# Experts with a second size of tail: 64 rows on two column groups of TensorE, beside 32 rows on four

## The reference

```python
logits = hf @ w_router + b_router;  top_val, top_idx = lax.top_k(logits, 4)
gu  = lax.ragged_dot(xs, w_gu, group_sizes) + b_gu[e]          # 1024 -> 2048
act = gate * sigmoid(1.702 * gate) * (up + 1)                  # gate and up clamped at 7
out = lax.ragged_dot(act, w_down, group_sizes) + b_down[e]     # 1024 -> 1024
y   = segment_sum(out * prob, token)
```

```
 79 155  99 160 155 146  93 132 | 134 122 191 150 161 127 214  96
129 100 143 124  64 152 147 122 | 114 152  91 115 122 105 162 168
```

## Time and profile before

| | us |
|---|---|
| median of three runs | 2581.58 |
| the profiled execution | 2580.96 |
| its span in the profile | 2579.4 |

### The profile page before, as it was taken

One profiled execution on the slowest core, in us unless ns is written; L12 is line 12 of the kernel. 1 busy time (PEld: TensorE's weight loads), 2 busy tenths in 40 slices (PEclk: granted clock), 3 DMA queues, 4 the chain that ended last, 5 costly groups with the idle time before them and its releaser, 6 DMA issues. The chain is left out here.

```text
span 2579.4 us, 36293 instructions
## 1 busy us (share of the span) xinstructions
PE 2373.8 (92%) x11130; PEld 1553.7 (60%) x11131; DVE 1391.8 (54%) x1996; ACT 1117.1 (43%) x1443; POOL 566.2 (22%) x843
## 2 busy tenths in 40 slices
PE   8589999999986399999999999999999999999965
PEld 1177677777754256556567566766575666676641
DVE  0124554545333566556466666766565575766647
ACT  0023333333221345445455455555454554555532
POOL 0122333333211312112112121221121212121110
PEclk9799999999687699999999999999999999999985
DMA  8840000000020787778689889988797797999945
GB/s 307 330 173 34 33 33 33 27 14 23 29 66 12 290 320 286 264 277 318 251 313 344 312 319 371 343 317 313 293 335 301 258 362 277 350 343 368 350 161 222
DMA packets 142977, 604.43 MB, mean 234 GB/s; under 512 B 20129, under 2 KB 25262, under 8 KB 104470
## 3 DMA queue, kind: packets, MB, share of 16 engines
q1 hardware_dynamic: 120311, 551.51, 55.0%
q0 software_dynamic: 21968, 50.99, 8.1%
q10 hardware_dynamic: 662, 1.50, 0.2%
HBM read 561.82 MB, written 42.30 MB: 234 GB/s over the span
## 5 line engine op out<-in xcount | busy, mean ns | idle before, releaser
L1710 DVE TENSOR_TENSOR lo<-raw,hi 128x1024 fp32r<-128x1024 f32 x600 | 716.6, 1222 | 200.1 <-ACT hi L1645 173.2
L1645 ACT ACTIVATE hi<-raw 128x1024 fp32r<-128x1024 f32 x600 | 613.1, 1054 | 172.4 <-PE pg L1595 172.4
L1529 PE MATMUL py<-raw,aT 128*128 128x512 f32 x1184 | 537.9, 599 | 6.3 <-ACT aT L1657 6.3
L1592 PE MATMUL pg<-hi,xs 128*128 128x512 f32 x1184 | 467.3, 395 | 0.0
L1593 PE MATMUL pg<-lo,xs 128*128 128x512 f32 x1184 | 465.3, 393 | 0.0
L1595 PE MATMUL pg<-hi,xs 128*128 128x512 f32 x1184 | 367.3, 392 | 0.0
L1529 PEld LDWEIGHTS py<-raw,aT 128*128 128x128 f32 x1184 | 214.5, 190 | 250.2 <-issue 238.0
L1592 PEld LDWEIGHTS pg<-hi,xs 128*128 128x128 f32 x1184 | 222.9, 188 | 68.9 <-issue 20.1
L1595 PEld LDWEIGHTS pg<-hi,xs 128*128 128x128 f32 x1184 | 222.8, 188 | 49.2
L1593 PEld LDWEIGHTS pg<-lo,xs 128*128 128x128 f32 x1184 | 223.1, 188 | 47.4
L392 PE MATMUL X<-hT,w_in 128*128 128x128 f32 (+1 forms) x1728 | 223.8, 289 | 0.8 <-issue 0.8
(11 more groups left out here) (295 smaller groups left out, 2581.0 us busy)
## 6 DMA issues: line engine op xcount, KB each, us to landing
raw<-in_w_gu SPq DMA_DIRECT2D x300, 1024.0 KB, 7.3
raw<-in_w_down SPq DMA_DIRECT2D x148, 1024.0 KB, 6.9
wada<-in_w_ada SPq DMA_DIRECT2D x12, 2048.0 KB, 7.7
w_in<-in_w_in SPq DMA_DIRECT2D x5, 2048.0 KB, 14.1
moe_rows<-zero SPq DMA_DIRECT2D x9, 512.0 KB, 11.6
x<-in_x_prompt SPq DMA_DIRECT2D x8, 512.0 KB
w_out<-in_w_out SPq DMA_DIRECT2D x1, 4096.0 KB, 25.0
xr<-in_x_prompt SPq DMA_DIRECT2D x8, 512.0 KB, 3.7
```

Of the source, the lines that this page charges most:

```text
L1529: return pe.matmul(py[n][:, :], aT[:, kt, :], raw[KT + kt // 2][:, kt % 2, n * 512:(n + 1) * 512], start=(kt == 0), stop=(kt == KT - 1))
L1592: pe.matmul(pg[u][b][:, :], xs[:, kt, 0, :], wh[:, u, :], start=False, stop=False)
L1645: act.activation(hi[q % RING][:, :, :], grain(q), ACT.Copy).then_inc(s["hi"], 1)
L1710: dve.tensor_tensor(lo[q % RING][:, :, :], grain(q), hi[q % RING][:, :, :].bitcast(F32), ALU.subtract).then_inc(s["lo"], 1)
```

## The change

`TAILS = (32, 64)`: a tail is of class 1 up to 32 rows and of class 2 up to 64, IDLE becomes 3. An expert with 161 to 192 rows is now one item. A 64-row tail runs on two column groups of 64: group g makes 512 gate columns into py0 and 512 up columns into py1, so there are two matmuls (u) for each group in bias and up-projection, and two of 512 columns for each kt of the down-projection. Every engine has a third body, chosen by a second comparison. GpSimd loads the tail's slots in both arrangements (four copies of 32, two of 64), keeps both, and gathers always 64 rows of the tail. `act_t` moves into the upper half of `act1`; three waits are added for that and for py1. Cut to its core:

```diff
-TAIL = 32
+TAILS = (32, 64)
+TAIL = max(TAILS)
...
-IDLE = 2
+IDLE = 1 + len(TAILS)
...
-            dve.tensor_scalar(ic[0:M, 9:10], ic[0:M, 5:6], float(ITEM + TAIL), None, ALU.is_gt).then_inc(s["im1"], 1)
+            dve.tensor_scalar(ic[0:M, 10:11], ic[0:M, 5:6], float(ITEM + TAILS[0]), None, ALU.is_gt)
+            dve.tensor_scalar(ic[0:M, 9:10], ic[0:M, 5:6], float(ITEM + TAIL), float(len(TAILS)), ALU.is_gt, ALU.mult).then_inc(s["im1"], 1)
             dve.wait_ge(s["im1"], 8)
+            dve.tensor_tensor(ic[0:M, 7:8], ic[0:M, 7:8], ic[0:M, 10:11], ALU.add)
             dve.tensor_tensor(ic[0:M, 8:9], ic[0:M, 8:9], ic[0:M, 9:10], ALU.subtract).then_inc(s["im1"], 1)
             dve.wait_ge(s["im1"], 9)
             dve.tensor_tensor(ic[0:M, 7:8], ic[0:M, 7:8], ic[0:M, 8:9], ALU.add).then_inc(s["im1"], 1)
...
+        xs_t = sb("xs_t", [P, KT * TAIL])
...
+        act_t = act1[:, 512:1024]
...
-                                body(i, False)
+                                body(i, 0)
                             with eng.Else():
-                                body(i, True)
+                                with eng.If(cls < 2):
+                                    body(i, TAILS[0])
+                                with eng.Else():
+                                    body(i, TAILS[1])
+
+        def part(T, u):
+
+            return slice(None) if T == TAILS[0] else u
+
+        def per_group(T):
+
+            return T * FF // P
...
+                for T, rows in zip(TAILS, (idx_t, idx_u)):
+                    for g in range(P // T):
+                        pool.dma_start(rows[g * T:(g + 1) * T, :], scratch["slots"][bass.ds(first + P, T), :]).then_inc(s["idx"], 16)
...
-                                        bass.IndirectOffsetOnAxis(ap=idx_t[0:TAIL, 0:1], axis=0)).then_inc(s["xg_t"], 16)
+                                        bass.IndirectOffsetOnAxis(ap=idx_u[0:TAIL, 0:1], axis=0)).then_inc(s["xg_t"], 16)
...
-                pool.tensor_copy(nxt_t[:, :], idx_t[:, :]).then_inc(s["nxt"], 1)
+                pool.tensor_copy(nxt_t[:, :], idx_t[:, :])
+                pool.tensor_copy(nxt_u[:, :], idx_u[:, :]).then_inc(s["nxt"], 1)
...
+                    pool.indirect_dma_start(scratch["acc"][:, :], bass.IndirectOffsetOnAxis(ap=now_u[0:tail, 1:2], axis=0),
+                                            act1[0:tail, :], None, compute_op=ALU.add).then_inc(s["y_out"], 16)
...
+            def tail_bias(T):
+                W = per_group(T)
+                for u in range(W // 256):
+                    for g in range(P // T):
+                        pe.matmul(py[u][g * T:(g + 1) * T, :], sel[:, 0:T].bitcast(F32),
+                                  bgu[:, :].rearrange("e (u n) -> e u n", u=2)[:, part(T, u), g * W:(g + 1) * W].bitcast(F32), start=True, stop=False)
+
+            def tail_up(kt, T):
+                W = per_group(T)
+                for u in range(W // 256):
+                    for g in range(P // T):
+                        last = pe.matmul(py[u][g * T:(g + 1) * T, :], xs_t[:, kt * T:(kt + 1) * T], raw[kt][:, part(T, u), g * W:(g + 1) * W],
+                                         start=False, stop=(kt == KT - 1))
                 return last
...
-                for c in range(2):
+                for c in range(per_group(T) // P):
                     last = pe.transpose(pg[0][0][:, c * P:(c + 1) * P], act_t[:, c * P:(c + 1) * P], identm[:, :])
...
+            def tail_down(kt, T):
+                W = per_group(T)
+                g, c = kt // (W // P), kt % (W // P)
+                for n in range(P // T):
+                    last = pe.matmul(pg[1][0][n * T:(n + 1) * T, 0:W], aT_t(T)[:, c, g * T:(g + 1) * T],
+                                     raw[KT + kt // 2][:, kt % 2, n * W:(n + 1) * W], start=(kt == 0), stop=(kt == KT - 1))
                 return last
...
+                    tail_rows(i, tail)
...
                         pe.wait_ge(s["xt"], i + 1)
                         pe.wait_ge(s["y0"], i + 1)
+                        pe.wait_ge(s["y1"], i + 1)
                         pe.sem_inc(s["met"], 1)
-                        tail_bias()
+                        tail_bias(tail)
...
+                    T, W = tail, per_group(tail)
+                    for n in range(P // T):
+                        last = act.activation(act1[0:T, n * W:(n + 1) * W], pg[1][0][n * T:(n + 1) * T, 0:W], ACT.Copy)
                     last.then_inc(s["y_t"], 1)
...
+                if tail and b:
+                    dve.wait_ge(s["aTt_ps"], i + 1)
...
+                gate_ps = py[0][:, 0:W]
+                up_ps = py[0][:, W:2 * W] if T == TAILS[0] else py[1][:, :]
+                weight = (now_t if T == TAILS[0] else now_u)[:, 2:3].bitcast(F32)
                 dve.wait_ge(s["gt_mm"], i + 1)
-                dve.tensor_scalar(gate[:, 0:W], py[0][:, 0:W], LIMIT, None, ALU.min).then_inc(s["gate_t"], 1)
-                dve.tensor_scalar(up[:, 0:W], py[0][:, W:2 * W], -LIMIT, LIMIT, ALU.max, ALU.min).then_inc(s["up_t"], 1)
+                dve.wait_ge(s["y_out"], i * 32 + 32)
+                dve.tensor_scalar(gate[:, 0:W], gate_ps, LIMIT, None, ALU.min).then_inc(s["gate_t"], 1)
+                dve.tensor_scalar(up[:, 0:W], up_ps, -LIMIT, LIMIT, ALU.max, ALU.min).then_inc(s["up_t"], 1)
...
-                dve.scalar_tensor_tensor(out=gate[:, 0:W], in0=gate[:, 0:W], scalar=now_t[:, 2:3].bitcast(F32), in1=sig[:, 0:W],
+                dve.scalar_tensor_tensor(out=gate[:, 0:W], in0=gate[:, 0:W], scalar=weight, in1=sig[:, 0:W],
                                          op0=ALU.mult, op1=ALU.mult).then_inc(s["glu_t"], 1)
...
-                dve.scalar_tensor_tensor(out=act_t[:, :], in0=up[:, 0:W], scalar=1.0, in1=gate[:, 0:W],
+                dve.scalar_tensor_tensor(out=act_t[:, 0:W], in0=up[:, 0:W], scalar=1.0, in1=gate[:, 0:W],
                                          op0=ALU.add, op1=ALU.mult).then_inc(s["act_t"], 1)
```

More of the change, by code:

```diff
@@ L1458, in load_slots @@
                 pool.dma_start(idx[:, :], scratch["slots"][bass.ds(first, P), :]).then_inc(s["idx"], 16)
-                for g in range(4):
-                    pool.dma_start(idx_t[g * TAIL:(g + 1) * TAIL, :], scratch["slots"][bass.ds(first + P, TAIL), :]).then_inc(s["idx"], 16)
+                for T, rows in zip(TAILS, (idx_t, idx_u)):
+                    for g in range(P // T):
+                        pool.dma_start(rows[g * T:(g + 1) * T, :], scratch["slots"][bass.ds(first + P, T), :]).then_inc(s["idx"], 16)
             def gather(item):
-                pool.wait_ge(s["idx"], item * 80 + 80)
+                pool.wait_ge(s["idx"], item * 112 + 112)
                 pool.sem_inc(s["met"], 1)
@@ L1535, in tail_rows @@
                 for kt in range(KT):
-                    last = pe.transpose(pt[0][:, kt * TAIL:(kt + 1) * TAIL], xg_t[:, kt * P:(kt + 1) * P], identm[0:TAIL, 0:TAIL])
+                    last = pe.transpose(pt[0][:, kt * T:(kt + 1) * T], xg_t[0:T, kt * P:(kt + 1) * P], identm[0:T, 0:T])
                 last.then_inc(s["xt_ps"], 1)
[L1539 to L1542, removed]
@@ L1553, in tail_act @@
                     last = pe.transpose(pg[0][0][:, c * P:(c + 1) * P], act_t[:, c * P:(c + 1) * P], identm[:, :])
                 last.then_inc(s["aTt_ps"], 1)
[L1556 to L1559, removed]
-                                     raw[KT + g][:, c, n * W:(n + 1) * W], start=(kt == 0), stop=(kt == KT - 1))
+            def tail_down(kt, T):
[4 more added lines that the diff above has]
+                                     raw[KT + kt // 2][:, kt % 2, n * W:(n + 1) * W], start=(kt == 0), stop=(kt == KT - 1))
@@ L1599, in item @@
                 if tail:
-                    tail_act(i)
+                    tail_act(i, tail)
                 transpose_rows(i + 1, 0)
@@ L1661, in item @@
                     act.wait_ge(s["xt_ps"], i + 1)
-                    act.activation(xs_t[:, :, :], pt[0][:, 0:KT * TAIL].rearrange("p (k t) -> p k t", k=KT), ACT.Copy).then_inc(s["xt"], 1)
+                    act.activation(xs_t[:, 0:KT * tail], pt[0][:, 0:KT * tail], ACT.Copy).then_inc(s["xt"], 1)
                 for q in range(RING, GRAINS):
@@ L1669, in item @@
                     act.wait_ge(s["gate_t"], i + 1)
-                    act.activation(sig[:, 0:W], gate[:, 0:W], ACT.Sigmoid, scale=ALPHA).then_inc(s["sig_t"], 1)
+                    act.activation(sig[:, 0:per_group(tail)], gate[:, 0:per_group(tail)], ACT.Sigmoid, scale=ALPHA).then_inc(s["sig_t"], 1)
                 squash(i, 0)
@@ L1676, in item @@
                     act.wait_ge(s["aTt_ps"], i + 1)
[L1677 removed]
+                    act.activation(aT_t(tail), pg[0][0][:, 0:per_group(tail)].rearrange("p (c t) -> p c t", t=P), ACT.Copy).then_inc(s["aT_t"], 1)
                 squash(i, 1)
@@ L1686, in item @@
                     act.wait_ge(s["yt_mm"], i + 1)
-                    for n in range(4):
```

(6 more changed lines are left out.)

45 lines of the change are left out of this document (20 added, 25 removed).

## The result

The changed kernel takes 2552.24 us (median of four, 2550.29 to 2555.35) against 2581.79 us (2580.42 to 2586.19): ratio 0.9884 [0.9867, 0.9901], 29.5 us less. Forecast were 2534.4 us and a range up to 2544. The profiled execution is the slowest of the four, 2555.35 us, span 2553.8.

What follows compares the result with a forecast made beforehand. TensorE was taken as the bound, with transfers close behind in plain items. Items -311.5 + 4 x 64.9 = -51.9 us, plus 1.0 start, 0.2 plan, 4.1 end: -46.6 from 2580.96 gives 2534.4 us, range 2527.5 to 2544.

Steps and rivals of the forecast that it cites:

- The 12 items with 32-row tails and the 17 plain ones I leave at their lengths: Expert phase: unchanged item classes stay at 53.09 and 38.94 us, since the second comparison runs ahead in TensorE's queue.
- My sign for stretches that have grown: Between GpSimd's stores: stretches of 53.1 or 38.9 us that have grown would prove the forecast wrong at the cover.
- the cover in the new item: 64-row item: VectorE's longer tail activation for b = 0 still ends 0.8 us before TensorE comes for it.
- The new item: Each of four 64-row items takes 64.9 us, between 64.5 and 65.3, with its two column groups running side by side.
- The 0.6 for wider copies and transpositions: 64-row item: 0.2 us each for more activation transpositions, wider row transpositions and ScalarE's wider copy.
- The bound of two groups in turn: 64-row item: groups run one after the other, 87.3 us an item and 2624 us in all; chance 5%.
- the stalls: New item: the cover fails or a copy is late by 1 to 3 us, adding 4 to 12 us; chance 11%.
- The rival in the prediction: Changes of item class: third body fetched at 19 changes, 7.1 us each, 135 us more, 2669 us; chance 1%.
- GpSimd ahead of the first item: Before the first gather: two more small transfers cost 0 to 3.9 us, taken as 1.0; hidden in later items.
- The end: Behind the last store: four more idle steps of 1.03 us, 4.1 us, with 0 as lower bound.
- The rival that gave it 22%: End of the phase: GpSimd's drain swallows the added idle steps, giving 2530.3 us; chance 22%.
- The first item and the plan: Start: two more plan operations cost 0.2 us; the first item was forecast to gain 0.

Runs made afterwards that it cites:

- e5: Changed kernel with xs alone moved back to 192 modulo 256, its remainder in the kernel before; 2540.64 us.
- e2: Kernel before with xs alone shifted by 32 bytes, by unused tensors before and behind it; 2595.95 us.
- e8: Kernel before with GpSimd's part of the change alone (64-row lists, copies, gather), xs kept at 192 modulo 256; 2580.95 us, ratio 0.9999.
- e3: Changed kernel with items walked in groups of 24 instead of 8, so 16 reads instead of 11 behind the last store; 2562.3 us.
- e6: Changed kernel with xs moved by pads to remainder 0 modulo 256; 2539.05 us in one profiled execution.
- e15: Changed kernel with xs at 0 modulo 256, run again and timed; 2534.43 us, ratio 0.9812.
- e1: Changed kernel with xs 32 bytes further, at a multiple of 64 bytes, by one unused tensor; 2552.09 us, ratio 0.9874.
- e10: Changed kernel with xs at 0 modulo 256, groups of 36, and the 128-row gather waiting for its own list only; 2521.99 us, ratio 0.9762.

## Why the prediction missed

**Which step failed.** "The 12 items with 32-row tails and the 17 plain ones I leave at their lengths." They grew by 0.37 to 0.40 us, which makes 12 x 0.38 = 4.6 us, 15 x 0.40 = 6.0 us, and 2.0 us for the one of 40.96: the whole gap of 12.6 us between the stores. I argued from instructions and waits, and both were right for these items, but for one stall (below); what changed was the address of an operand, which no view of the profile and no line of the diff about matmuls shows. By the sums of the stretches in the changed kernel and in e5 the address is worth 1532.54 - 1520.55 = 12.0 us, the four new items with it; the stall and a new item priced too high nearly cancel in what is left. My sign for stretches that have grown pointed at the cover in the new item, and it was not that. e2 puts it into the kernel before, e5 takes it out of the changed one. Where it acts can be seen in both traces: from the bias of a plain item to the transposition of its activation stand 1590.93 - 1569.85 = 21.08 us before and 1654.78 - 1633.32 = 21.46 after. That is the whole 0.38, over the 90 matmuls of the up-projection between them 4 ns each (the other six of an item's 96 stand ahead of this bias).

```profile
1569.85 0.63 PE L1578 MATMUL pg<-bgu,sel 128*128 128x512 f32 x2
...
1590.93 0.60 PE L1525 MATMUL pt<-ident,actm 128*128 128x128 f32 x4
```

```profile
1633.32 0.63 PE L1604 MATMUL pg<-bgu,sel 128*128 128x512 f32 x2
...
1654.78 0.60 PE L1546 MATMUL pt<-ident,actm 128*128 128x128 f32 x4
```

(Before, then after; each in order of time.)

**Items: right.** 33 stores, with expert 10 among the four, as counted.

**The new item: right in kind, its number by luck.** 64.9 us forecast, 64.88 to 64.94 measured; but at the distance of before it is 64.53 to 64.59 (e5). The sum over a plain item was 22.4 + 3.0 + 0.6 = 26.0 us; it is 64.53 - 38.94 = 25.6. The 0.6 for wider copies and transpositions was too much by 0.4, and the place put 0.38 back. The bound of two groups in turn, 87.3 us, is refuted, as are the stalls: cover 0.96 us where I gave 0.8. The share of the transfers is 0.63 where I gave 0.56, with TensorE busy in all but 0.4 us of the stretch.

**The third body: one stall, once.** A stall of 1.35 us stands where TensorE first leaves a body with a tail for the plain one:

```profile
983.97 0.70 PE L1604 MATMUL pg<-bgu,sel 128*128 128x512 f32 x2 [1.35 <-issue]
```

The item costs 40.96 - 39.37 = 1.6 us over a later plain one behind a tail, once. Every kernel with the third body has the stall at this place, 1.0 to 1.8 us long, and none without it. It is a fetch of instructions, by the times of the packets on that queue (24 of 16 KB in the changed kernel, 18 before). One starts at 982.8 us and takes 0.88; TensorE's first load of the plain body, after 2.15 us of standing idle, is at 983.94. From there to the end of the phase only three more come, at 1374.9, 1395.4 and 1422.0, all in the first item with a 64-row tail, and they delay nothing that shows; the kernel before and e8 have none after 925.0 and 925.8 until the phase is over. The trace doesn't say whose instructions a packet holds; but by their times a fetch comes with the first entry into a body and with the first return to the plain one, and never again. The rival in the prediction had the mechanism, but 19 times and at 7.1 us. All later changes of class cost at most 0.06 us: 39.37 behind a tail, 39.31 behind none. The Trainium skill (Runtime: NRT & Kernel Launch, Instruction fetch mechanics) would have a stall at each branch out of the two pages held; this trace shows it at the first only.

**GpSimd ahead of the first item.** Forecast 1.0 with 0 to 3.9, measured 1.9 (e8 alone: 1.9). The issue was right, at 1.07; "transfers in flight together mostly land together" was not quite: the wait grew by 0.75 us.

**The end.** Forecast 4.1, came 9.1. Two terms were mis-sized. An idle step costs 1.17 us, not 1.03, and seven were right: with the steps about them 5.6 us. Why a step is longer stays open: in e8, without the third body, an idle item still takes 1.03 us but an idle group 1.18. The other 3.4 us are the drain, which I had as fixed or as shrinking, and which grew. The rival that gave it 22%, that it swallows the steps, falls by e3.

**The first item and the plan.** 2.3 and 0.7 us over. The 0.7 I don't account for: the plan's table came between 853.3 and 859.2 us in kernels whose engines do nearly the same work ahead of it. Of the 2.3, some 0.4 are the place. Most of the rest stands in a wait for the rows of the second item, 1.67 us, where the kernel before has none and only waits 0.25 us for ScalarE just behind:

```profile
913.53 0.66 PE L1540 MATMUL pt<-ident,xg 128*128 128x128 f32 x4 [1.67 <-DMA xg<-h_rows,idx]
```

It is not a fixed cost of the change: e6 and e15 are one kernel, took 53.25 and 49.54 us for the first item, and waited 2.67 and 0.88 us here; e1 has no such wait.

**The range.** All its upper reach, 2544, was for stalls in the new item. No case had a cost spread over all the items that stay, though 29 of them times a few tenths was the largest lever in the sum; and the start alone scatters by some 6 us (the plan's table above). At distance 192 the kernel takes 2540.64 us in a single execution (e5), inside the range. That e15 gives 2534.43, the very forecast, is chance: it has a better place than the kernel before and a worse end than I gave it.

## What to carry to other kernels

A change that makes or removes a small tensor moves every tensor behind it; so compare the addresses of TensorE's operands modulo 256 bytes before one explains a new item length, and keep the distance with padding when two versions are compared. In a sum over many equal stretches, give the ones "left as they are" a bound too: their number multiplies a small error. And a wait for several transfers that feed different readers is worth splitting where an engine stands still behind it: e10 got 2526.95 - 2521.99 = 5.0 us that way, of which its trace shows 4.7 at the first gather.

## What the runs showed of the hardware

- Matmuls of 512 columns in fp32r, one after the other, start 227 ns apart with stationary and moving operand at the same remainder modulo 256 bytes, 229 ns apart with a distance of 192, and 233 ns with 32, 64, 128 or 224. Items of 38.74, 38.93 and 39.33 us (39.22 at 128) belong to these; from 192 to 224 it was 13.6 us in the kernel before (e2), 0.5%. What in the chip makes it so is not shown.
- Two groups of 64 columns take a pass of 512 columns in 0.43 us, as four of 32 do: a tail of 64 rows costs 25.6 us, one of 32 rows 14.15.
- GpSimd's drain at the end of the phase took 2.52 to 9.54 us in kernels that differ in transfers issued long before, and did not change with 0, 5 or -7 reads more in front of it.
- In a loop over three bodies the instruction queue moved packets at the first entry into each and at the first return to the plain one: one stall of 1.35 us, then 17 changes of body that cost at most 0.06 us.
- A step over an idle item costs GpSimd's queue 1.03 us in the kernel before and 1.17 in the changed one, behind the last store in full.
